# A down projection of mixture-of-experts blocks of at most 256 rows with its operands' roles exchanged

## Chip, cores and metric

The kernel runs on one core of a Trainium2 chip. The metric is the device time of one execution in microseconds (us); the profile is of one execution on that core.

## The reference

A block of a language model on 2048 tokens of width 1024. Three mixing branches (windowed attention, retention, attention to a memory) are computed, gated, merged and projected, and added to the input. What the change is about comes last:

```
logits = ht @ w_router + b_router                # 2048 tokens, 32 experts
top_vals, top_idx = lax.top_k(logits, 4)
gate = softmax(top_vals)
hid = ragged_dot(xs, w_up, group_sizes) + b_up   # 1024 -> 2048 per expert, rows sorted by expert
x_glu = minimum(hid[:, 0::2], 7.0)
x_lin = clip(hid[:, 1::2], -7.0, 7.0)
act = x_glu * sigmoid(1.702 * x_glu) * (x_lin + 1.0)
out = ragged_dot(act, w_down, group_sizes) + b_down      # 1024 -> 1024 per expert
y = zeros.at[tok].add(out * gate)
```

All of it is float32. Each product is formed from two parts of each operand, a high part rounded to the matmul's type (`_hi`) and the rest (`_lo`), in three passes: hi x hi, lo x hi and hi x lo.

## The kernel before

The kernel is a row of stages with a barrier between them. `project_mixers` projects the branches, `finish_mixing` finishes the mixing, routes the tokens and plans the blocks, and `run_experts` computes the experts from about 2356 us to the end.

**Blocks.** `finish_mixing` sorts the (token, expert) rows by expert, cuts each expert's rows into blocks of at most 384 (three tiles of 128) and sorts the blocks by size into seven width classes, `WIDTHS` (224, 240, 256, 272, 288, 304, 384). For each block a row of the table `blocks` holds the expert, the number of live tiles (`LIVE`), the first row, the number of tiles in the blocks before (`PRIOR`); the ends of the classes are in it too. `each_block` makes one loop for each class, so that the code of a block knows its width.

**One block on TensorE** (`pe`, from line 2650). A unit is a weight tile of 256 rows (`KU` = 2 chunks of 128) by 256 columns, 256 KB. A pair n is a group of 256 weight columns and has 4 units, m = 0 to 3. Pairs 0 to 7 (`UP` = 8) are the up projection, pairs 8 to 11 the down projection, 48 units in all. `unit` (lines 2630 to 2632) holds a 128 x 128 piece of the weights stationary and moves the block's rows, `width` columns at a time: 12 matmuls in a unit, results in two of the four banks `acc`, with output channels on the partitions. After the down projection, ScalarE adds the bias while it evicts a bank to `yT` (`take_down`, line 2427), TensorE turns `yT` back into rows (`turn_y`, line 2607, 4 transposes for a tile and half), and ScalarE multiplies them by the gate into `ys` (`gate`, line 2435). Half 0 (512 output channels) of a block is turned in pairs 10 and 11 of the same block, half 1 in pairs 0 and 1 of the next. POOL adds `ys` to the output by indirect DMAs (`scatter`).

**The next block's rows.** POOL gathers them into `xg`. TensorE turns them tile by tile into the one PSUM buffer `xT` (`turn_x`, line 2598, 8 transposes), ScalarE makes `x_hi` from it (line 2409), VectorE `x_lo` (line 2509). `turn_x` of tile i waits for `x_lo` of tile i - 1. The calls stand behind pair n = 7 (tile 0), n = 8 (tile 1) and n = 9 (tile 2):

```
if UP - 1 <= n < UP + 2:
    turn_x(following, n - UP + 1)
```

**The weights.** SyncE loads units in order into 8 raw buffers (`load`, line 2305), each as soon as the split eight units before it is done. ScalarE makes the high part `w_hi` (`split`, line 2403), VectorE `w_lo` (line 2503). 16 units are held (`HELD`); unit u goes where unit u - 16 was, and ScalarE waits for it by the semaphore `used`, which TensorE raises after each unit. In program order both engines split four pairs ahead: beside pair n they handle the units of pair n + 4, or those of the next block. When the up projection ends, all 16 units of the down projection fill the 16 places.

**The order on the engines** is written out by hand. VectorE for an up pair (from line 2561): read the first bank (`open_glu`, line 2514), split, read the second (`open_lin`, 2519), multiply by the sigmoid, split, multiply, split, the low part of the activations (`split_a`, 2536), split. ScalarE: split, sigmoid, two splits, `a_hi`, split. Both do `x` of tile 0 behind all eight pairs, and tiles 1 and 2 behind the third unit of pairs 8 and 9. TensorE's first matmul into a bank waits until the bank has been read (`free_bank`).

**Other places touched.** At the start of the stage POOL clears `yT` (line 2378) and ScalarE waits for it. In `project_mixers` ScalarE casts four weight chunks and then the first input tile (line 1578). In `finish_mixing` VectorE makes the columns of the table and TensorE sorts them.

## Time and profile before

| what | us |
|---|---|
| median of 3 runs (lowest to highest) | 4849.71 (4848.52 to 4853.77) |
| the profiled execution | 4852.9 |
| its span, first to last instruction | 4851.2 |

The profile gives for each engine its busy time: PE is TensorE's matmuls, PEld its weight loads, which overlap them, DVE VectorE, ACT ScalarE, POOL GpSimd; SPq is SyncE's queue of DMA issues. The timeline gives start, duration, engine, line, operation, output<-inputs, count, and in brackets the idle time of the engine before the instruction and what ended it. Matmuls overlap, so the distance between their starts is their price, and not their duration. PEclk is TensorE's granted clock as a share of 2.4 GHz.

### The profile page before, as it was taken

The page shows a single profiled execution, that of the slowest core. Times are in us where ns is not written, and L with a number is a line of the kernel's source. Part 1 is how long each engine was busy: PE and PEld are TensorE (multiplying, and loading weights), DVE is VectorE, ACT ScalarE, POOL GpSimd, SP SyncE. Part 2 cuts the span into 40 slices and gives each one's busy share as a digit, 9 for nine tenths or more (in the row PEclk, how much of TensorE's full clock was granted, in tenths as well). Part 3 has the DMA queues.
Part 4 walks back from the last instruction along what each step waited for, and adds up shares of the span by engine and source line. Part 5 has one row for each costly group of instructions (what it writes and reads, how often), then busy time and mean ns, then how long its engine had stood idle before and what let it go on. Part 6 is the DMA issues. An engine that isn't in the chain of part 4 may idle for free.

```text
span 4851.2 us, 98702 instructions
## 1 busy us (share of the span) xinstructions
PE 4650.1 (96%) x31230; PEld 4328.0 (89%) x31231; DVE 2937.2 (61%) x5403; ACT 2108.5 (43%) x3853; POOL 472.6 (10%) x455
## 2 busy tenths in 40 slices
PE   7999999999699899989699999999999999999997
PEld 6888888888477778878699999999999999999997
DVE  6555565555388644355566766666666666565654
ACT  4222221221377631222355555555555555555553
POOL 3000000000133100012200010001010110101000
PEclk9999999999799999999799999999999999999999
DMA  5333343232344443444476777676675767665654
GB/s 190 106 118 102 128 148 112 100 106 86 144 160 159 160 152 137 157 158 138 149 212 202 223 220 214 190 216 210 187 216 175 226 182 215 182 208 176 203 165 113
DMA packets 573959, 806.10 MB, mean 166 GB/s; under 512 B 51216, under 2 KB 516624, under 8 KB 566800
## 3 DMA queue, kind: packets, MB, share of 16 engines
q1 hardware_dynamic: 548032, 718.01, 45.1%
q0 software_dynamic: 25808, 86.59, 7.4%
q8 instruction: 65, 1.06, 0.1%
q14 instruction: 54, 0.44, 0.0%
HBM read 650.25 MB, written 154.21 MB: 166 GB/s over the span
## 4 chain that ended last, share of the span: by engine, by line
PE 50%; DMA 1%; DVE 0%; issue 0%; SPq 0%; ACT 0%; DVEq 0%; POOLq 0%; ACTq 0%
PE e_acc L2632 16%; PE e_acc L2630 16%; PE e_acc L2631 16%; PE e_xT L2598 2%; PE e_yp L2607 1%; DMA e_raw<-in_w_up 1%; DMA out<-e_ys,e_rec_out 0%; DVE e_wlo L2503 0%; DVEq L2254 0%; DVE e_xlo L2509 0%; ACT e_whi L2403 0%; SPq L2305 0%; POOLq L2198 0%; DVE e_lin L2519 0%; ACT e_ys L2435 0%
## 5 line engine op out<-in xcount | busy, mean ns | idle before, releaser
L2503 DVE TENSOR_TENSOR e_wlo<-e_raw,e_whi 128x512 fp32r<-128x512 f32 x1552 | 1055.7, 688 | 545.8 <-ACT e_whi L2403 529.2
L2630 PE MATMUL e_acc<-e_xhi,e_whi 128*128 128x272 f32 (+6 forms) x4096 | 1182.3, 289 | 3.6 <-DVEq L2558 2.6
L2632 PE MATMUL e_acc<-e_xlo,e_whi 128*128 128x272 f32 (+6 forms) x4096 | 1178.3, 288 | 0.0
L2631 PE MATMUL e_acc<-e_xhi,e_wlo 128*128 128x272 f32 (+6 forms) x4096 | 1176.6, 287 | 0.0
L2403 ACT CAST e_whi<-e_raw 128x512 fp32r<-128x512 f32 x1552 | 951.5, 647 | 196.8 <-DMA e_raw<-in_w_up 160.0
L2630 PEld LDWEIGHTS e_acc<-e_xhi,e_whi 128*128 128x128 f32 x4096 | 774.0, 189 | 4.6 <-issue 3.0
L2631 PEld LDWEIGHTS e_acc<-e_xhi,e_wlo 128*128 128x128 f32 x4096 | 775.6, 189 | 0.0
L2632 PEld LDWEIGHTS e_acc<-e_xlo,e_whi 128*128 128x128 f32 x4096 | 773.4, 189 | 0.0
L606 PE MATMUL p_acc<-p_hi,a_hi 128*128 128x464 f32 x1792 | 670.0, 374 | 6.9 <-DVE p_lo L508 6.9
L608 PE MATMUL p_acc<-p_hi,a_lo 128*128 128x464 f32 x1792 | 669.0, 373 | 0.0
L607 PE MATMUL p_acc<-p_lo,a_hi 128*128 128x464 f32 x1792 | 666.6, 372 | 0.0
L2630 PE MATMUL e_acc<-e_ahi,e_whi 128*128 128x272 f32 (+6 forms) x2048 | 598.9, 292 | 0.0
L2632 PE MATMUL e_acc<-e_alo,e_whi 128*128 128x272 f32 (+6 forms) x2048 | 588.6, 287 | 0.0
L2631 PE MATMUL e_acc<-e_ahi,e_wlo 128*128 128x272 f32 (+6 forms) x2048 | 587.5, 287 | 0.0
L475 ACT CAST p_hi<-p_raw 128x928 fp32r<-128x928 f32 x192 | 176.7, 969 | 638.7 <-PE p_acc L608 635.7
L2631 PEld LDWEIGHTS e_acc<-e_ahi,e_wlo 128*128 128x128 f32 x2048 | 387.5, 189 | 0.0
L2630 PEld LDWEIGHTS e_acc<-e_ahi,e_whi 128*128 128x128 f32 x2048 | 386.6, 189 | 0.0
L2632 PEld LDWEIGHTS e_acc<-e_alo,e_whi 128*128 128x128 f32 x2048 | 386.1, 189 | 0.0
L606 PEld LDWEIGHTS p_acc<-p_hi,a_hi 128*128 128x128 f32 x1792 | 336.9, 188 | 46.9 <-issue 7.1
L608 PEld LDWEIGHTS p_acc<-p_hi,a_lo 128*128 128x128 f32 x1792 | 336.6, 188 | 42.7
L607 PEld LDWEIGHTS p_acc<-p_lo,a_hi 128*128 128x128 f32 x1792 | 336.8, 188 | 40.8
L533 DVE TENSOR_TENSOR p_u<-p_acc,p_u 128x464 f32<-128x464 f32 x320 | 197.0, 638 | 262.5 <-PE p_acc L608 262.5
(331 smaller groups left out, 6247.0 us busy)
## 6 DMA issues: line engine op xcount, KB each, us to landing
e_raw<-in_w_up SPq DMA_DIRECT2D x1040, 256.0 KB, 3.2
e_raw<-in_w_down SPq DMA_DIRECT2D x512, 256.0 KB, 4.6
p_raw<-in_w_in SPq DMA_DIRECT2D x64, 928.0 KB, 4.9
z<-p_z SPq DMA_DIRECT2D x32, 928.0 KB, 4.0
z<-p_u SPq DMA_DIRECT2D x32, 928.0 KB, 3.9
b_gates<-z SPq DMA_DIRECT2D x16, 1536.0 KB, 7.0
oT<-x_oT SPq DMA_DIRECT2D x16, 1024.0 KB, 9.6
b_raw<-oT SPq DMA_DIRECT2D x16, 1024.0 KB, 9.6
```

The costliest lines, as they stand in the source:

```text
L475: act.copy(w_hi[slot(b, j)][:, ks, :], operand[j][:, ks, :]).then_inc(hi_made.sem, 1)
L533: dve.tensor_tensor(out[:, q, :], acc[slot(b, j)][q][:, 0:G], other[:, q, :], ALU.add).then_inc(added.sem, 1)
L606: pe.matmul(out, a_hi[:, j, at], hi[:, k, :], start=k == 0, stop=False)
L607: pe.matmul(out, a_hi[:, j, at], lo[:, k, :], start=False, stop=False)
L608: mm = pe.matmul(out, a_lo[:, j, at], hi[:, k, :], start=False, stop=k == HALF_K - 1)
L2403: act.copy(held(w_hi, u), loaded(u)).then_inc(hi_made.sem, 1)
L2503: dve.tensor_tensor(held(w_lo, u), loaded(u), held(w_hi, u).bitcast(F32), ALU.subtract).then_inc(lo_made.sem, 1)
L2598: mm = pe.transpose(xT[:, k * P:(k + 1) * P], xg[i][:, k * P:(k + 1) * P], ident[:])
L2607: mm = pe.transpose(yp[i % 2][:, j * P:(j + 1) * P], yT[half][:, j, i * P:(i + 1) * P], ident[:])
L2630: pe.matmul(out, whi, hi[:, k, 0:width], start=k == 0, stop=False)
L2631: pe.matmul(out, wlo, hi[:, k, 0:width], start=False, stop=False)
L2632: mm = pe.matmul(out, whi, lo[:, k, 0:width], start=False, stop=k == KD - 1)
```

## The change

For classes of at most 256 rows (`narrow`) the down projection holds the activations stationary (128 x 128 pieces of `a_hi` and `a_lo`, the last piece as wide as the rows left) and moves 512 weight columns, taken from two units at once (`rows_part`). One part is 12 matmuls and uses units m of two pairs. Its results have rows on the partitions: four banks, one for each half and tile. VectorE adds the bias row, which SyncE broadcasts by DMA to all partitions once a block (`add_row`, into `ya`), and ScalarE multiplies by the gate into `ys` (`gate_rows`). No `take_down` and no `turn_y` is done for these blocks; TensorE raises `y_turned` at the block's end instead. `used` rises by one behind each of the first three parts of a half and by five behind the fourth. `turn_x` of tiles 1 and 2 stands behind the first and second part. The table has a new column `LATE`, the live tiles of a block of the wider classes and 0 for a narrow one, which tells the next block whether transposes of half 1 are owed. POOL clears `ys`, and ScalarE waits for that. In `project_mixers` ScalarE waits, before it casts the first input tile, until the last outputs of the stage before are written. The diff, cut to its core:

```diff
@@ -1579,6 +1579,9 @@
 
             for n in range(KO):
                 if n == PARTS[0][1]:
+
+                    for written in weights.outputs_written:
+                        act.wait_ge(written.sem, written.after(TILES // 2 - 1))
                     split(0, 0, 0)
...
@@ -1685,10 +1688,12 @@
-EXPERT, LIVE, FIRST, COUNT, PRIOR, CUTS = range(6)
+EXPERT, LIVE, FIRST, COUNT, PRIOR, LATE, CUTS = range(7)
 WIDTHS = (224, 240, 256, 272, 288, 304, BLOCK_TILES * P)
 CLASSES = len(WIDTHS)
+NARROW = 3
+assert WIDTHS[NARROW - 1] <= 2 * P
...
+            link(dve.tensor_scalar(val[:, LATE:LATE + 1], over[:, NARROW:NARROW + 1], live, None, ALU.mult), False)
...
+        ya = sb("ya", [P, 2, 2, HALF])
+        down_row = sb("down_row", [P, D])
...
+        row_in, ys_cleared = sig("row_in", 16), sig("ys_cleared")
+        NARROW_TAKEN = ((3, 6), (7, 8))
...
-                if column == LIVE:
-                    self.live = self.get(LIVE, BLOCK_TILES)
+                if column == LIVE or column == LATE:
+                    self.live = self.get(column, BLOCK_TILES)
...
+                        sp.wait_ge(y_taken.sem, y_taken.after(b, 0))
+                        stand(sp, idle)
+                        sp.dma_start(down_row[:], io["b_down"][ds(e, 1), :].to_broadcast([P, D])).then_inc(row_in.sem, 16)
...
+            for t in ys:
+                pool.memset(t[:], 0.0).then_inc(ys_cleared.sem, 1)
...
+            def gate_rows(b, block, half, i, width):
+
+                rows = min(width - i * P, P)
+                act.wait_ge(y_taken.sem, y_taken.after(b, NARROW_TAKEN[half][i]))
+                act.wait_ge(rec_kept.sem, block.row)
+
+                act.wait_ge(y_sent.sem, block.prior * 16)
+                act.activation(ys[i][0:rows, half * HALF:(half + 1) * HALF], ya[0:rows, half, i, :], ACT.Copy,
+                               scale=rec_now[0:rows, i, 1:2].bitcast(F32)).then_inc(y_gated.sem, 1)
...
+            act.wait_ge(ys_cleared.sem, BLOCK_TILES)
...
+                narrow = width <= 2 * P
+                now = Block(act, b + 1)
+                if not narrow:
+                    before = Block(act, b, LATE, PRIOR)
                 for n in range(UP):
-                    if n == 0:
+                    if n == 0 and not narrow:
                         with before.tile(0):
                             gate(before, 1, 0)
                         with before.tile(1):
                             gate(before, 1, 1)
-                    if n == 1:
+                    if n == 1 and not narrow:
...
+                if narrow:
+                    stand(act, down_kept)
+                    for half in range(2):
+                        for m in range(PARTS - 1):
+                            split(*ahead(b, UP + 2 * half, m))
+                            if half == 0 and m < BLOCK_TILES - 1:
+                                with following.tile(m + 1):
+                                    split_x(following, m + 1, used.after(b, UP * PARTS))
+                        if half == 1:
+                            for i in range(2):
+                                with now.tile(i):
+                                    gate_rows(b, now, 0, i, width)
+                        split(*ahead(b, UP + 2 * half, PARTS - 1))
+                        if half == 1:
+                            for i in range(2):
+                                with now.tile(i):
+                                    gate_rows(b, now, 1, i, width)
+                        for m in range(PARTS):
+                            split(*ahead(b, UP + 2 * half + 1, m))
+                    continue
...
+            def add_row(b, half, i, width):
+                rows = min(width - i * P, P)
+                if i == 0:
+                    dve.wait_ge(summed.sem, summed.after(b, UP + 2 * half + 2))
+                else:
+                    dve.wait_ge(used.sem, used.after(b, (UP + 2 * half + 2) * PARTS))
+                dve.tensor_tensor(ya[0:rows, half, i, :], acc[2 * half + i][0:rows, :],
+                                  down_row[0:rows, half * HALF:(half + 1) * HALF], ALU.add).then_inc(
+                                      y_taken.sem, NARROW_TAKEN[half][i] - (NARROW_TAKEN[half][i - 1] if i else 6 * half))
...
+                if width <= 2 * P:
+                    dve.wait_ge(row_in.sem, row_in.after(b))
+
+                    dve.wait_ge(y_gated.sem, now.prior * 2 + 1)
+                    stand(dve, idle)
+                    for half in range(2):
+                        for m in range(PARTS - 1):
+                            split(*ahead(b, UP + 2 * half, m))
+                            if half == 0 and m < BLOCK_TILES - 1:
+                                with following.tile(m + 1):
+                                    split_x(following, m + 1)
+                        if half == 0:
+                            dve.wait_ge(x_lo_made.sem, following.prior + following.live + 1)
+                            dve.sem_inc(x_ready.sem, 1)
+                        for i in range(2):
+                            add_row(b, half, i, width)
+                        split(*ahead(b, UP + 2 * half, PARTS - 1))
+                        for m in range(PARTS):
+                            split(*ahead(b, UP + 2 * half + 1, m))
+                    continue
...
+            def rows_part(b, half, m, width):
+
+                for u in (UP + 2 * half, UP + 2 * half + 1):
+                    pe.wait_ge(lo_made.sem, lo_made.after(b, u * PARTS + m + 1))
+                first = 2 * half * PARTS + m
+                for kk in range(KU):
+                    k = m * KU + kk
+                    whi, wlo = (w[:, first:first + PARTS + 1:PARTS, kk, :] for w in (w_hi, w_lo))
+                    for i in range(2):
+                        if k == 0:
+                            free_bank(b, UP + half, i)
+                        cols = slice(i * P, min(width, (i + 1) * P))
+                        out = acc[2 * half + i][0:cols.stop - cols.start, :]
+                        hi, lo = a_hi[:, k, cols], a_lo[:, k, cols]
+                        pe.matmul(out, hi, whi, start=k == 0, stop=False)
+                        pe.matmul(out, hi, wlo, start=False, stop=False)
+                        mm = pe.matmul(out, lo, whi, start=False, stop=k == KD - 1)
+                        if k == KD - 1 and i == 0:
+                            mm.then_inc(summed.sem, 2)
+                mm.then_inc(used.sem, 1 if m < PARTS - 1 else PARTS + 1)
...
+                narrow = width <= 2 * P
                 pe.wait_ge(x_ready.sem, b + 1)
-                for n in range(PAIRS):
-                        if n == 0 and m == 1:
+                        if n == 0 and m == 1 and not narrow:
                             before = Block(pe, b, PRIOR)
-                        if n == 0 and m == 2:
-                            before.load(LIVE)
+                        if n == 0 and m == 2 and not narrow:
+                            before.load(LATE)
...
-                        if n == 0 and m == 3:
+                        if n == 0 and m == 3 and not narrow:
                             turn_y(before, 1, 0, y_taken.after(b, 0))
                             turn_y(before, 1, 1, y_taken.after(b, 0))
-                        if n == 1 and m == 2:
+                        if n == 1 and m == 2 and not narrow:
                             turn_y(before, 1, 2, y_taken.after(b, 0))
...
+                if narrow:
+                    for half in range(2):
+                        for m in range(PARTS):
+                            if half == 0:
+                                pe.wait_ge(a_lo_made.sem, a_lo_made.after(b, (m + 1) * KU))
+                            rows_part(b, half, m, width)
+                            if half == 0 and m < BLOCK_TILES - 1:
+                                turn_x(following, m + 1)
+                    for i in range(2):
+                        with now.tile(i):
+                            pe.sem_inc(y_turned.sem, 2)
```

## Rows read from the trace of the kernel before

**Rows 1.** The page, busy time and share of the span of each engine

```profile
PE 4650.1 (96%) x31230; PEld 4328.0 (89%) x31231; DVE 2937.2 (61%) x5403; ACT 2108.5 (43%) x3853; POOL 472.6 (10%) x455
```

**Rows 2.** Windows of the experts' stage: busy time, count, PEclk, DMA share

```profile
core 0: us, PE busy (x) PEld busy (x) DVE busy (x) ACT busy (x) POOL busy (x), PEclk, DMA share, GB/s
2380.00:4785.00 2405.00, 2404.03 (x19474) 2401.33 (x19474) 1564.02 (x2912) 1342.30 (x2549) 228.50 (x220) 1.00 0.67 201
```

**Rows 3.** Groups by form, up projection: count, busy us, mean ns

```profile
L2630 PE MATMUL e_acc<-e_xhi,e_whi 128*128 128x240 f32 x896 | 247.4, 276 | 0.0
...
L2630 PE MATMUL e_acc<-e_xhi,e_whi 128*128 128x256 f32 x640 | 181.2, 283 | 0.0
...
L2630 PE MATMUL e_acc<-e_xhi,e_whi 128*128 128x224 f32 x384 | 107.1, 279 | 3.3 <-DVEq L2558 2.6 <-DVE e_lin L2519 0.4 <-DVE e_glu L2514 0.3
```

**Rows 4.** Windows with matmuls alone, of 224, 240, 256 and 512 columns

```profile
2467.00:2492.00 25.00, 25.00 (x226) 25.00 (x226) 20.30 (x44) 14.54 (x30) 1.84 (x2) 1.00 0.90 280
2740.00:2765.00 25.00, 25.00 (x223) 25.00 (x223) 20.07 (x43) 13.84 (x28) 1.79 (x2) 1.00 0.90 284
3158.00:3183.00 25.00, 25.00 (x211) 25.00 (x210) 19.06 (x40) 13.44 (x27) 1.91 (x2) 1.00 0.90 277
1820.00:1920.00 100.00, 100.00 (x432) 80.58 (x431) 39.48 (x51) 18.71 (x8) 0.00 (x0) 1.00 0.40 140
```

**Rows 5.** Timeline of PE around the transposes of the outputs: start, us, line

```profile
3004.30 0.27 PE L2632 MATMUL e_acc<-e_xlo,e_whi 128*128 128x240 f32 x1
3004.41 1.04 PE L2607 MATMUL e_yp<-ident,e_yT 128*128 128x128 f32 x8
3005.20 0.36 PE L2630 MATMUL e_acc<-e_xhi,e_whi 128*128 128x240 f32 x1
3005.40 0.28 PE L2631 MATMUL e_acc<-e_xhi,e_wlo 128*128 128x240 f32 x1
```

**Rows 6.** Timeline of PE where a down projection of 240 columns begins

```profile
2974.40 1.04 PE L2598 MATMUL e_xT<-ident,e_xg 128*128 128x128 f32 x8
2975.19 0.36 PE L2630 MATMUL e_acc<-e_ahi,e_whi 128*128 128x240 f32 x1
...
2980.60 0.27 PE L2632 MATMUL e_acc<-e_alo,e_whi 128*128 128x240 f32 x1
2980.85 1.09 PE L2598 MATMUL e_xT<-ident,e_xg 128*128 128x128 f32 x8
```

**Rows 7.** Timelines of ACT and DVE in the same stretch

```profile
2978.52 1.02 ACT L2409 CAST e_xhi<-e_xT 128x1024 fp32r<-128x1024 f32 x1 [0.63 <-PE e_acc L2632]
...
2979.57 1.23 DVE L2509 TENSOR_TENSOR e_xlo<-e_xT,e_xhi 128x1024 fp32r<-128x1024 f32 x1 [0.95 <-ACT e_xhi L2409]
```

**Rows 8.** Timeline of PE in the last mixing stage, around an idle time

```profile
2092.45 1.03 PE L2131 MATMUL f_mT<-ident,f_mg 128*128 128x128 f32 x8
2096.05 0.47 PE L334 MATMUL f_acc<-f_whi,f_mhi 128*128 128x512 f32 x1 [2.56 <-DVE f_mlo L1969]
```

**Rows 9.** Window behind that idle time, columns as in rows 2

```profile
2096.80:2100.20 3.40, 3.40 (x9) 2.63 (x8) 2.22 (x12) 0.77 (x2) 0.00 (x0) 0.50 0.39 154
```

**Rows 10.** Timeline of DVE at the start of a block

```profile
3005.57 0.17 DVE L2565 COPY e_up_bias<-e_bias 128x16 f32 x1 [3.48 <-issue]
3005.88 0.47 DVE L2514 TENSOR_SCALAR e_glu<-e_acc,e_up_bias 128x240 f32<-128x240 f32 x1
```

**Rows 11.** Timeline at the start of the experts' stage

```profile
2362.41 2.71 POOL L2378 MEMSET e_yT<- 128x1536 f32 x2
...
2366.62 0.65 ACT L2403 CAST e_whi<-e_raw 128x512 fp32r<-128x512 f32 x1 [8.88 <-issue]
...
2371.08 1.01 ACT L2409 CAST e_xhi<-e_xT 128x1024 fp32r<-128x1024 f32 x1
```

**Rows 12.** DMA issues between 1689 and 1691 us, last number us to landing

```profile
oT<-x_oT SPq DMA_DIRECT2D x1, 1024.0 KB, 4.2
```

**Rows 13.** Timeline of ACT at the opening of the projection of the mixers

```profile
1697.92 1.90 ACT L1578 CAST b_ohi<-b_raw 128x2048 fp32r<-128x2048 f32 x1 [2.51 <-DMA b_raw<-oT]
```

More of the change, by code:

```diff
@@ L2451, in _ @@
             for b, width in each_block(act):
-                before, now = Block(act, b), Block(act, b + 1)
+                narrow = width <= 2 * P
+                now = Block(act, b + 1)
+                if not narrow:
+                    before = Block(act, b, LATE, PRIOR)
                 for n in range(UP):
-                    if n == 0:
+                    if n == 0 and not narrow:
                         with before.tile(0):
@@ L2475, in _ @@
                     down_kept.sem, 1)
-                act.wait_ge(down_kept.sem, b + 1)
+                act.wait_ge(down_kept.sem, down_kept.after(b))
                 for n in range(UP, PAIRS):
@@ L2650, in _ @@
             for b, width in each_block(pe):
+                narrow = width <= 2 * P
                 pe.wait_ge(x_ready.sem, b + 1)
-                for n in range(PAIRS):
+                for n in range(UP if narrow else PAIRS):
                     for m in range(PARTS):
-                        if n == 0 and m == 1:
+                        if n == 0 and m == 1 and not narrow:
                             before = Block(pe, b, PRIOR)
-                        if n == 0 and m == 2:
-                            before.load(LIVE)
+                        if n == 0 and m == 2 and not narrow:
+                            before.load(LATE)
                         if n == 2 and m == 0:
```

## The prediction

> **What bounds the kernel now.** I read the page's busy line first, then the windows, then the groups by form, then the timeline around one block. The page has TensorE busy 96% of the span [rows 1]. The windows sharpen this: from 2380 to 4785 us the experts' stage runs, and TensorE is busy 2404.0 of 2405 us at the full clock (2.4 GHz), VectorE 65% and ScalarE 56%, DMA at 0.67 [rows 2]. So every microsecond taken from or added to TensorE's own sequence there moves the end, and work of the other engines counts only where TensorE comes to wait for it.
>
> How many blocks does the change touch? An up projection issues 128 matmuls of each of its three lines per block, and the groups of line 2630 have 384, 896 and 640 of them at 224, 240 and 256 columns [rows 3]: 3, 7 and 5 blocks, 15 of the 32. The wider 17 keep their path.
>
> **Part A, the matmuls.** A narrow block's down projection is now 8 column groups x 8 chunks x 3 passes = 192 matmuls of `width` moving columns; it becomes 2 halves x 8 chunks x 2 row tiles x 3 = 96 of 512. The price is the distance from start to start. Four windows in which nothing but matmuls runs give it [rows 4]; each count holds about two that straddle the edges. 25 us / 224 = 111.6 ns at 224 columns, 25 / 221 = 113.1 at 240, 25 / 209 = 119.6 at 256, and 100 us / 430.5 = 232 ns at 512 columns (stage before, same three passes, stationary 128 x 128, full clock). New: 96 x 232 = 22.27 us. Old: 21.43, 21.72, 22.96. The differences are +0.84 x 3, +0.55 x 7, -0.69 x 5 = +2.9 us. Halving the number of matmuls buys nothing, because the columns streamed are 49,152 against 43,008 to 49,152.
>
> A rule of the Trainium skill speaks for much more: TensorE: Matmul & The Clock Gate, section "Back-to-back issue gap", puts a sustained stream of weight load and matmul at about 131 ns for 512 columns, and by it the 96 would take 12.6 us and the kernel would gain over 100 us. The row at 512 columns says 232, so the sum stands as above.
>
> **Part B, the transposes of the outputs.** They go for narrow blocks: one pair of tiles (8 transposes) for half 0 and one for half 1, the latter in the next block. One pair: last matmul at 3004.30, transposes at 3004.41, the next matmuls at 3005.20 and 3005.40, where two steps of 0.113 would have done [rows 5]: 1.10 - 0.23 = 0.87 us. 30 x 0.87 = -26.1 us, all of it on the bounding engine. ScalarE's gates had waited for these; they are replaced by as many gates from SBUF.
>
> **Part C, a transpose of the next block's rows that comes too early.** Transposing input tile i needs the one xT buffer, so it waits for `x_lo` of tile i-1. Tile 0 is turned at the end of the up projection (2974.40), the down projection starts at 2975.19, and tile 1 is turned behind pair n = 8, at 2980.85 [rows 6]. In the new order tile 1 is turned behind `rows_part(0, 0)`, that is behind 12 matmuls: 2975.19 + 0.09 + 12 x 0.232 = 2978.06. What must be there is `x_lo` of tile 0: ScalarE makes x_hi at 2978.52 to 2979.54, VectorE x_lo at 2979.57 to 2980.80 [rows 7]. Both stand behind the last gate chain and the last weight splits of the up projection, in the order that the change leaves as it is. So TensorE waits from 2978.06 to 2980.85, 2.79 us. Today's order just fits: its last matmul started 2980.60, a wait of 0.14. Net +2.65. The other blocks repeat this: the turn of tile 1 stands 5.58 to 5.67 us behind the first down matmul in all ten blocks of 224 and 240, and in the five of 256 x_lo is ready 5.65 to 5.67 behind it. That gives +2.58 (224), +2.65 (240), +2.84 (256); 3, 7 and 5 times: +40.5 us. Nothing hides it, since TensorE has no other work in its queue behind the waiting transpose. This is the largest term.
>
> **Part D, the clock.** Before each turn TensorE would stand 2.5 us without work, and with the transposes there are 3.5 us between matmuls. The nearest row is in the stage before: transposes from 2092.45, then idle 2.56 us, matmuls from 2096.05 [rows 8]; then 3.4 us in which the granted clock is 0.50 (1.2 GHz, the lower level) and only 8 whole matmuls fit, 0.42 each instead of 0.232 [rows 9]. Lost: 3.4 - 8 x 0.232 = 1.54 us. That gap and mine are alike (3.6 us between matmuls there). Ends: never 0, every time 15 x 1.54 = 23 us. One row can't say how often; I take every second time, +11.5. The same page of the Trainium skill, in its table "Why this matters for your kernels", warns only of idle gaps longer than these; by that the term would be 0, but the row shows a fall behind one of 2.56 us.
>
> **Small parts.** Bias row: SyncE issues one more DMA per block (512 KB beside 12 MB of weights) behind unit 23 of the up projection, waiting for the previous block's last bank to be read, long done by then; VectorE needs the row some 25 us later, so 0. Behind it on SyncE's queue stand the loads of units 24 and on, eight units ahead of their split. VectorE gains four adds of 512 columns per block (each about as long as one of the 48 weight splits, also 512 columns) and ScalarE loses eight evictions; VectorE is 65% busy. The last two adds fall at the block's end, together with five splits that the new credits of `used` release at once. VectorE then reaches the next block's first bank late: today 3005.88, 6.9 us into the block (whose 48th matmul is the one at 3004.30), after 3.48 us in which it only loads registers [rows 10]; with two adds more and the splits bunched there I estimate two us more, some 9.1. TensorE needs that bank at pair 2, 10.8 us in, and its second at 11.2, which VectorE frees at about 10.6. The cover is about half a microsecond; 0 taken, up to +0.5 per block kept. TensorE's two `sem_inc` per block have no row; between 0 (the sequencer runs ahead) and one transition like the 0.09 above each, +2.7 in all; 0 taken. Start of the stage: POOL clears ys too, three tiles of 1024 columns, as many as the two of 1536 that took 2.71 us, and ScalarE waits for it; its first cast goes from 2366.62 to about 2369.3, but the three casts behind it waited for weights anyway, so x_hi at 2371.08 slips by only about 0.6 [rows 11]. With the planner's extra operation and column, +1.0. The new wait at the opening of the projection of the mixers: the last 1 MB of outputs is issued between 1689 and 1691 and lands 4.2 us later, by 1695.2 [rows 12], and ScalarE stands idle at this place for 2.51 us, until 1697.92, for another DMA [rows 13]: 0, at most +1 if the two waits should add.
>
> **Sum.** +2.9 - 26.1 + 40.5 + 11.5 + 1.0 = +29.8 us. The profiled execution is 4852.9 (span 4851.2), 3.2 above the median of the three runs (4849.7); against the median that gives 4879.5.
>
> **Rivals.**
> - *The clock holds.* Same stalls, term D at 0: +18.3, 4868. For it: a turn of 8 transposes ends each gap, and one row is thin. Against: that same row. Chance 0.22.
> - *The next block's first banks come late too*, or the clock falls every time. VectorE's backlog at the block's end outgrows its half microsecond, or 15 falls: +36 to +50, 4886 to 4900. Chance 0.15.
> - *Faster: the stall isn't there.* If x_lo of tile 0 were ready before 2978.06, or the turn cost TensorE nothing, A, B and the start alone would remain: 2.9 - 26.1 + 1.0 = -22.2, 4827.5. It decides by the wait: with no clock loss, the break-even is a net wait of 22.2 / 15 = 1.5 us per block instead of 2.65. For it: VectorE idles 0.95 us ahead of x_lo. Against: that idling is for ScalarE's x_hi, and ScalarE's sequence ahead of x_hi is untouched and starts when the up projection ends. A second way to this side is the 512 columns streaming faster from the two-part weight tile: at 213 ns, 96 x 19 ns x 15 = -27 us. Chance together 0.09.
> - *No change*, a wait half as long or the faster stream against the stalls: within 9.7 us. Chance 0.06.
> - That the new path isn't taken can be left out: the counts at three widths say it is, in 15 blocks.
>
> **How the numbers follow.** The forecast (stalls with the clock falling at part of them) has 0.48. This kernel's measurement can tell 0.2% (9.7 us) from no change. Slower by more: 0.48 + 0.22 + 0.15 = 0.85; within: 0.06; faster: 0.09. The range must hold 8 in 10: from the clock holding, less a few us for the rate of 512 columns (232 might be 229 in this stage, -4), to falls every time with some of the small terms: 4863 to 4896. It leaves out the faster side, the no-change cases and the far end of the late banks.
>
> **What would show it.** Right: TensorE in the experts' stage no longer at 100%; a wait of the transposes on `x_lo` of some 2.8 us, 15 times, about 42 us in the list of waits; matmuls of 512 columns 0.232 us apart; TensorE at half clock for a few us behind some of the waits; a narrow block's down phase near 26 us against 23.7 for 240 columns, its up phase 0.87 shorter. Wrong: no such wait (then A and B stand alone and the kernel is faster), 512 columns off 232 ns, or waits on VectorE's reads of the first banks of a block.

## The result, and the profile after

The changed kernel takes 4927.6 us (median of 5 runs, 4925.1 to 4935.4) against 4852.4 for the kernel before, run beside it: a ratio of 1.0158, with a 95% interval of 1.0147 to 1.0169, or 75 us more. The forecast was slower by 29.8 us, 4879.5, with a range of 4863 to 4896. The direction was right, the size was not, and the result lies outside the range. The profiled execution has a span of 4924.6 us, 73.4 more than the one before.

The page first, its busy line:

```profile
PE 4653.9 (95%) x29552; PEld 4243.8 (86%) x29553; DVE 2968.5 (60%) x5464; ACT 2062.1 (42%) x3718; POOL 483.6 (10%) x458
```

TensorE's busy time hardly changed against [rows 1] (4650.1), so the time went into idle time. Windows of the experts' stage say where, the 15 narrow blocks first and the 17 wide ones behind them. The columns are those of [rows 2].

```profile
core 0: us, PE busy (x) PEld busy (x) DVE busy (x) ACT busy (x) POOL busy (x), PEclk, DMA share, GB/s
2380.00:3472.00 1092.00, 1048.53 (x7443) 965.76 (x7443) 747.62 (x1430) 571.14 (x1051) 95.13 (x88) 0.98 0.70 210
3472.00:4860.00 1388.00, 1361.01 (x10363) 1354.22 (x10362) 847.92 (x1543) 724.71 (x1362) 140.34 (x132) 1.00 0.65 195
```

Before, TensorE was busy 2404.0 of 2405 us. Now it stands 43 us in the narrow blocks, and 27 in the wide ones, whose code on TensorE the change left alone. From the first matmul of the first narrow block to that of the first wide one it takes 3472.38 - 2378.66 = 1093.7 us against 1052.8, +40.9; from there to the end of the span it is 1452.2 against 1419.6, +32.6. The two make up the 73.4. TensorE's own list of waits, from 2390 to 4800 us, names two causes (us in total, times, longest):

```profile
PE e_xT L2678 <- DVE e_xlo L2559: 39.6, 15, 2.9
PE e_acc L2731 <- DVE e_lin L2569: 30.0, 34, 1.7
```

**The wait on x_lo** is part C. The timeline of TensorE in a block of 240 columns, where [rows 6] shows the kernel before:

```profile
2998.53 0.48 PE L2713 MATMUL e_acc<-e_whi,e_ahi 128*128 128x512 f32 x1
...
3001.17 0.40 PE L2715 MATMUL e_acc<-e_whi,e_alo 128*112 128x512 f32 x1
3004.16 1.09 PE L2678 MATMUL e_xT<-ident,e_xg 128*128 128x128 f32 x8 [2.60 <-DVE e_xlo L2559]
3005.01 0.48 PE L2713 MATMUL e_acc<-e_whi,e_ahi 128*128 128x512 f32 x1
```

The twelfth matmul of the first part starts at 3001.17, 2.64 us behind the first, and the transposes of tile 1 start at 3004.16: 5.63 us behind the first matmul, as in every block before (5.58 to 5.67 at these widths). The wait is 2.60 us by the profile, 15 such waits add up to 39.6 us.

**The clock.** This is another block of 240 columns, and then a window in it:

```profile
2928.76 0.40 PE L2715 MATMUL e_acc<-e_whi,e_alo 128*112 128x512 f32 x1
2931.77 1.97 PE L2678 MATMUL e_xT<-ident,e_xg 128*128 128x128 f32 x8 [2.61 <-DVE e_xlo L2559]
2933.39 0.78 PE L2713 MATMUL e_acc<-e_whi,e_ahi 128*128 128x512 f32 x1
2933.97 0.63 PE L2714 MATMUL e_acc<-e_wlo,e_ahi 128*128 128x512 f32 x1
...
2935.07 0.40 PE L2714 MATMUL e_acc<-e_wlo,e_ahi 128*112 128x512 f32 x1
```

```profile
2932.00:2935.00 3.00, 3.00 (x12) 2.69 (x12) 0.49 (x2) 1.01 (x1) 0.00 (x0) 0.53 0.30 94
```

The same wait, but then eight transposes take 1.62 us until the next matmul instead of 0.85, and matmuls stand 0.42 to 0.58 apart instead of 0.232, until about 2934.8; the granted clock of the window is 0.53, so most of it ran at the lower level, 1.2 GHz. Eleven of the fifteen narrow down phases show it, with a granted clock of 0.94 over the phase: two of 224 columns, four of 240 (27.5 to 27.6 us against 25.9 and 26.1 without) and all five of 256. Four do not (1.00). The expectation of `later` below says ten; the trace of the changed kernel has eleven.

**The wide blocks** were the surprise. Here is SyncE's queue in the up projection of a block of 272 columns, in the changed kernel and then at the same place in the kernel before:

```profile
3644.27 0.37 SPq L2320 DMA_DIRECT2D e_rec_in<-slots  x1
3645.00 0.34 SPq L2346 DMA_DIRECT2D e_down_row<-in_b_down  x1
3645.59 10.19 SPq L2315 DMA_DIRECT2D e_raw<-in_w_up  x8
```

```profile
3600.99 0.37 SPq L2310 DMA_DIRECT2D e_rec_in<-slots  x1
3601.62 5.35 SPq L2305 DMA_DIRECT2D e_raw<-in_w_up  x8
```

SyncE stands at this place until POOL has taken over the records, in both kernels. Its own list of waits in the wide blocks of the kernel before has:

```profile
SPq L2331 <- POOL e_rec_now L2387: 168.6, 17, 13.9
```

The loads behind it, held back, then go out at once. In the changed kernel the broadcast goes ahead of them: the first load is issued 1.32 us behind the records instead of 0.63, and the eight loads take 10.2 us to issue instead of 5.4. In the other blocks of 272 to 304 columns behind the first it is 7.6 to 10.7 against 5.1 to 8.5. ScalarE and TensorE, some 10 us later:

```profile
3646.41 0.67 ACT L2419 CAST e_whi<-e_raw 128x512 fp32r<-128x512 f32 x1
3655.43 0.64 ACT L2419 CAST e_whi<-e_raw 128x512 fp32r<-128x512 f32 x1 [8.35 <-DMA e_raw<-in_w_up]
```

```profile
3657.26 0.39 PE L2731 MATMUL e_acc<-e_xhi,e_whi 128*128 128x272 f32 x1 [1.14 <-DVE e_lin L2569]
```

ScalarE waits 8.35 us for the first of these weight tiles. In these fifteen blocks its longest wait for one is 7.5 to 8.4 us, before 2.0 to 3.8. Over all the wide blocks its list of waits has, before and after (us in total, times, longest):

```profile
ACT e_whi L2403 <- DMA e_raw<-in_w_up: 127.6, 82, 3.8
```

```profile
ACT e_whi L2419 <- DMA e_raw<-in_w_up: 183.6, 57, 8.4
```

So ScalarE stood for these loads before the change too, and TensorE didn't; now it stands 56 us longer, and some of it reaches TensorE. VectorE's split stands behind ScalarE's cast, and its reading of the second bank (`open_lin`) behind that split, so TensorE waits for the bank. An up projection of 272 columns takes 51.4 to 53.8 us instead of 50.3 to 51.0. In the first wide block (49.5 us against 49.8) and the last, of 384 columns (69.15 in both), no loss shows.

### The profile page after: what moved, and what is told of

It is laid out like the page before. It is cut to its first block, busy times and chain, and to the rows that moved or that the text cites. A ratio compares the mean times of both kernels' runs of the same rounds, so it can differ in the third digit from the quotient of the medians.

```text
span 4924.6 us, 94881 instructions
## 1 busy us (share of the span) xinstructions
PE 4653.9 (95%) x29552; PEld 4243.8 (86%) x29553; DVE 2968.5 (60%) x5464; ACT 2062.1 (42%) x3718; POOL 483.6 (10%) x458
## 4 chain that ended last, share of the span: by engine, by line
PE 41%; DMA 4%; DVE 2%; issue 2%; ACT 1%; DVEq 1%; SPq 1%; ACTq 0%; POOL 0%; POOLq 0%
PE e_acc L2731 11%; PE e_acc L2733 11%; PE e_acc L2732 11%; DMA e_raw<-in_w_up 4%; PE e_acc L2713 2%; PE e_acc L2714 2%; PE e_acc L2715 2%; PE e_xT L2678 1%; PE e_yp L2687 1%; DVEq L2264 1%; DVE e_wlo L2553 1%; SPq L2315 0%; ACT e_whi L2419 0%; DVE e_xlo L2559 0%; DVE e_lin L2569 0%
## 5 line engine op out<-in xcount | busy, mean ns | idle before, releaser
L2731 PE MATMUL e_acc<-e_ahi,e_whi 128*128 128x272 f32 (+3 forms) x1088 | 328.8, 302 | 0.0
L2733 PE MATMUL e_acc<-e_alo,e_whi 128*128 128x272 f32 (+3 forms) x1088 | 322.0, 296 | 0.0
L2732 PE MATMUL e_acc<-e_ahi,e_wlo 128*128 128x272 f32 (+3 forms) x1088 | 321.7, 296 | 0.0
L508 DVE TENSOR_TENSOR p_lo<-p_raw,p_hi 128x928 fp32r<-128x928 f32 x192 | 207.2, 1121 | 91.8 <-ACT p_hi L475 91.8
L2429 ACT ACTIVATE e_sg<-e_glu 128x272 f32<-128x272 f32 (+6 forms) x256 | 109.6, 428 | 289.6 <-DVE e_glu L2564 289.6
L334 PE MATMUL b_acc<-b_hi,b_ohi 128*128 128x512 f32 x512 | 203.1, 397 | 17.6 <-DVE b_olo L1609 16.0
```

The lines of the kernel that those rows point to most:

```text
L334: pe.matmul(out, x_hi(k), w_hi(k), start=first, stop=False)
L508: dve.tensor_tensor(w_lo[slot(b, j)][:, ks, :], operand[j][:, ks, :], w_hi[slot(b, j)][:, ks, :].bitcast(F32), ALU.subtract).then_inc(lo_m ...
L2731: pe.matmul(out, whi, hi[:, k, 0:width], start=k == 0, stop=False)
L2732: pe.matmul(out, wlo, hi[:, k, 0:width], start=False, stop=False)
L2733: mm = pe.matmul(out, whi, lo[:, k, 0:width], start=False, stop=k == KD - 1)
```

## Experiments

All times are medians; ratios are to the kernel before in the same job. Differences to the changed kernel are between medians of different jobs, in which the kernel before had 4851.1 to 4853.0 us, so they are good to a microsecond or two. The diffs are cut to their core: the runs that start from the kernel before also declare `down_row` and its semaphore, and before_tiny also waits for the last of these DMAs at the end of the program.

**before_row: the kernel before, plus the broadcast.**

```diff
                         load_records(b + 2)
+                        sp.wait_ge(y_taken.sem, y_taken.after(b, 0))
+                        stand(sp, idle)
+                        sp.dma_start(down_row[:], io["b_down"][ds(e, 1), :].to_broadcast([P, D])).then_inc(row_in.sem, 16)
```

> The kernel before, with one thing of the change added: SyncE's broadcast of the bias row (512 KB) behind unit 23 of every block; nobody reads it. In the changed kernel the 17 wide blocks, whose code on TensorE is the old one, take 32.6 us more from the first wide up projection to the end of the span (1419.6 to 1452.2 us), all of it in their up projections, where SyncE's eight held-back weight loads stand behind this DMA. Theory 'broadcast': this kernel loses the same, +30 to +38 us, in the wide blocks, and at most +5 in the 15 narrow ones. Rival 'something else of the change' (register loads, the LATE column, buffers at other addresses): within 5 us of before.

4885.5 against 4851.2, ratio 1.0067 (1.0050 to 1.0084): +34 us. The narrow blocks are as before to a tenth (45.2 us up, 23.7 to 23.8 down at 240 columns), and seven of the eight up projections at 272 columns take 52.0 to 53.6. From the first wide block to the end it is 1455.4 us, 35.9 more than before; some 3 of these belong to one block of 288 columns (57.6 us against 54.8 in the others), in which the clock also fell. TensorE's waits in the wide blocks:

```profile
PE e_acc L2636 <- DVE e_lin L2525: 19.8, 21, 1.7
PE e_acc L2636 <- issue: 5.1, 4, 1.5
```

The one DMA, read by nobody, reproduces the whole loss of the wide blocks. In the narrow blocks the same DMA costs nothing. Why was not tested by a run of its own, but the traces show a difference. By the code, SyncE is let go after two tiles of gathered rows there instead of three. In the kernel before it passes the place 8.7 to 9.1 us into a narrow block (11.5 in the first), and 14.2 to 15.5 us into a wide one of 272 to 304 columns. Two such blocks begin at 2930.01 and 3586.78:

```profile
2938.84 0.37 SPq L2310 DMA_DIRECT2D e_rec_in<-slots  x1
```

```profile
3600.99 0.37 SPq L2310 DMA_DIRECT2D e_rec_in<-slots  x1
```

One wide block is let go early too, the first one, at 9.4 us. It loses nothing by the broadcast (49.81 us up in both kernels). That speaks for the time at which SyncE gets there and against the width, but no run shows it. (The last block, of 384 columns, is let go at 18.5 us and loses nothing either; its up projection lasts 69 us.)

**narrow_row: the changed kernel, broadcast in narrow blocks only.**

```diff
-                        sp.wait_ge(y_taken.sem, y_taken.after(b, 0))
-                        stand(sp, idle)
-                        sp.dma_start(down_row[:], io["b_down"][ds(e, 1), :].to_broadcast([P, D])).then_inc(row_in.sem, 16)
+                        with sp.If(now.get(LATE, BLOCK_TILES) < 1):
+                            sp.wait_ge(y_taken.sem, y_taken.after(b, 0))
+                            stand(sp, idle)
+                            sp.dma_start(down_row[:], io["b_down"][ds(e, 1), :].to_broadcast([P, D])).then_inc(row_in.sem, 16)
```

> The changed kernel with the broadcast only in the blocks that read it (LATE is 0). Theory 'broadcast': the wide blocks' up projections return to 50.6 us at 272 columns (53.5 in the changed kernel), and the time falls by 30 to 36 us, to about 4894. Rival 'something else of the change': stays at about 4927.

4903.6, ratio 1.0104 (1.0088 to 1.0121): 24 us off the changed kernel, not 33. Behind the first wide block the up projections at 272 columns take 50.6 to 52.0. From the first wide block to the end it is 1430.8 us, still 11.3 more than before. Only the register load and the branch are left at this place, and they put the first held-back load off from 0.63 us behind the issue of the records to 1.48 or 1.49:

```profile
3562.49 0.37 SPq L2320 DMA_DIRECT2D e_rec_in<-slots  x1
3563.97 5.61 SPq L2315 DMA_DIRECT2D e_raw<-in_w_up  x8
```

The rest of the change is in the wide blocks of `moved` below as well, and those lose nothing. So the loads have no slack here, whatever it is that delays them.

**before_tiny: the kernel before, plus a DMA of 4 KB at that place.**

```diff
                         load_records(b + 2)
+                        sp.wait_ge(y_taken.sem, y_taken.after(b, 0))
+                        stand(sp, idle)
+                        sp.dma_start(down_row[0:1, :], io["b_down"][ds(e, 1), :]).then_inc(row_in.sem, 16)
```

> The kernel before with a DMA of the bias row to one partition (4 KB) at the place where the broadcast (512 KB) stood in before_row, and nothing else. If the broadcast costs by the data it moves ahead of the eight held-back weight loads, this is near 0 to +8 us (the issue alone: SyncE reaches the loads about 0.6 us later in each of 17 wide blocks). If it costs by anything that stands between SyncE's release and the loads, +30 us as in before_row. The run narrow_row, whose wide blocks had only a register load and a branch there, and no DMA, lost 11.2 us in them, so I expect between: +5 to +15.

4860.0 against 4851.1, ratio 1.0017 (1.0007 to 1.0027): +8.8 us, of which TensorE's list of waits in the wide blocks shows this:

```profile
PE e_acc L2637 <- DVE e_lin L2526: 4.9, 5, 1.3
```

Here the first held-back load is issued 1.26 us behind the records, 0.63 later than before, and from the first wide block to the end it is 7.0 us more. So a delay of the loads alone costs about a quarter of before_row's loss at 0.63 us and a third at the 0.86 of narrow_row. The rest comes with what the broadcast has more than the small DMA: 512 KB ahead of eight loads of 256 KB, in more packets.

**before_moved: the kernel before, plus the full broadcast behind unit 39.**

```diff
                         load_records(b + 2)
+                    if u == 10 * PARTS - 1:
+                        sp.wait_ge(y_taken.sem, y_taken.after(b, 0))
+                        stand(sp, idle)
+                        sp.dma_start(down_row[:], io["b_down"][ds(e, 1), :].to_broadcast([P, D])).then_inc(row_in.sem, 16)
```

> The kernel before with the full broadcast in every block, but behind unit 39 (the last of up pair 5's span of the queue), where the held-back loads have caught up. Theory 'it stands ahead of loads that have no slack': within 3 us of before, against +34 in before_row. Rival 'it costs DMA time wherever it stands': +15 to +34.

4851.7 against 4851.1, ratio 1.0002 (0.9993 to 1.0011). The same bytes in the same blocks, 16 units further on in the queue, cost nothing, and TensorE shows no wait in the wide blocks. The loss is one of place. The part of the expectation that named an up pair for the place was loose: unit 39 is a down unit in the queue, and its DMA is issued 28 to 41 us into a block, while TensorE is in the up projection.

**moved: the changed kernel, broadcast behind unit 39.** The edit is the one line `if u == 10 * PARTS - 1:` ahead of the three of the broadcast.

> The changed kernel with the broadcast behind unit 39 instead of unit 23, still in every block. The wide blocks return to their times of before (50.6 us for an up projection at 272 columns), the waits on x_lo and the falls of the clock stay: 32 to 36 us off, about 4893. If narrow blocks need the row sooner than that, VectorE waits on row_in and the narrow down phases grow.

4890.4, ratio 1.0085 (1.0069 to 1.0100): 37 us off the changed kernel. The up projections at 272 columns are back at 50.4 to 50.8, and the narrow down phases are unchanged (25.9 to 28.2 before the last), so the row arrives in time. Again eleven of them fall to the lower clock, but in part other blocks of 240 columns.

**later: the changed kernel, tiles 1 and 2 of the next block one part later.**

```diff
-                            if half == 0 and m < BLOCK_TILES - 1:
-                                with following.tile(m + 1):
-                                    split_x(following, m + 1, used.after(b, UP * PARTS))
+                            if half == 0 and m > 0:
+                                with following.tile(m):
+                                    split_x(following, m, used.after(b, UP * PARTS))
...
-                            if half == 0 and m < BLOCK_TILES - 1:
-                                with following.tile(m + 1):
-                                    split_x(following, m + 1)
+                            if half == 0 and m > 0:
+                                with following.tile(m):
+                                    split_x(following, m)
...
-                            if half == 0 and m < BLOCK_TILES - 1:
-                                turn_x(following, m + 1)
+                            if half == 0 and 0 < m < BLOCK_TILES:
+                                turn_x(following, m)
```

The three places are ScalarE's, VectorE's and TensorE's programs.

> The changed kernel with the transposes of the next block's tiles 1 and 2, and the two engines' splits of them, one part later (behind the second and third part of half 0). Theory 'too early': the wait on x_lo (43.8 us in 16 waits) goes, and with it the ten stretches at half clock in the narrow blocks; a 240-column block's down phase goes from 26.1 or 27.5 us to 23.4 to 23.6. -40 - 15 us: about 4872. Rival 'the wait only moves', to the third part or to the next block's start: 4900 to 4927.

4869.3, ratio 1.0037 (1.0022 to 1.0051): 58 us off the changed kernel, where 55 were expected. The transposes now follow the 24th matmul without a wait, and no narrow down phase runs at half clock:

```profile
2770.47 0.40 PE L2714 MATMUL e_acc<-e_wlo,e_ahi 128*128 128x512 f32 x1
2770.71 0.40 PE L2715 MATMUL e_acc<-e_whi,e_alo 128*128 128x512 f32 x1
2770.94 0.40 PE L2713 MATMUL e_acc<-e_whi,e_ahi 128*112 128x512 f32 x1
2771.18 0.39 PE L2714 MATMUL e_acc<-e_wlo,e_ahi 128*112 128x512 f32 x1
2771.41 0.40 PE L2715 MATMUL e_acc<-e_whi,e_alo 128*112 128x512 f32 x1
2771.64 1.07 PE L2678 MATMUL e_xT<-ident,e_xg 128*128 128x128 f32 x8
2772.47 0.48 PE L2713 MATMUL e_acc<-e_whi,e_ahi 128*128 128x512 f32 x1
```

A down phase of 240 columns takes 23.3 us, the up projections stay at 44.5 to 45.3.

**filler: the changed kernel with 11 matmuls inside the wait.**

```diff
                             rows_part(b, half, m, width)
+                            if half == 0 and m == 0:
+                                pe.wait_ge(lo_made.sem, lo_made.after(b, (UP + 1) * PARTS + 2))
+                                for _ in range(11):
+                                    pe.matmul(yp[0][:], a_hi[:, 0, 0:P], w_hi[:, 1:PARTS + 2:PARTS, 0, :], start=True, stop=True)
                             if half == 0 and m < BLOCK_TILES - 1:
                                 turn_x(following, m + 1)
```

> The changed kernel with 11 extra matmuls of 512 columns (results unused, 2.55 us) inside TensorE's wait of 2.79 us ahead of the transpose of tile 1. The end of the wait is set by x_lo and stays. Theory 'idle time drops the clock': no stretch at half clock in the narrow blocks' down phases, all of them 26.0 us instead of 26.1 or 27.5: -15 us, about 4912. Rival 'the clock falls for another reason, or its fall costs nothing on the path': 4925 to 4930.

4912.0, ratio 1.0122 (1.0105 to 1.0139): 15.5 us off the changed kernel, with more work in it. The wait on x_lo is filled, and what follows runs at full clock:

```profile
2926.66 0.39 PE L2715 MATMUL e_acc<-e_whi,e_alo 128*112 128x512 f32 x1
2926.89 2.74 PE L2795 MATMUL e_yp<-e_whi,e_ahi 128*128 128x512 f32 x11
2929.64 1.09 PE L2678 MATMUL e_xT<-ident,e_xg 128*128 128x128 f32 x8
2930.49 0.48 PE L2713 MATMUL e_acc<-e_whi,e_ahi 128*128 128x512 f32 x1
2930.80 0.39 PE L2714 MATMUL e_acc<-e_wlo,e_ahi 128*128 128x512 f32 x1
```

All narrow down phases of 224 and 240 columns are 25.9 to 26.1 us, those of 256 are 26.3 to 27.2 (27.9 to 28.8 in the changed kernel). In the traces the narrow blocks take 15.8 us less than in the changed kernel and their down phases 16.6 less, some 1.5 us for each of the eleven falls. That is the clock's share: a down phase without a fall is as long in both kernels (26.1 us at 240 columns).

**moved_later: both repairs.** The edits of moved and later together.

> Both repairs in the changed kernel: the broadcast behind unit 39, and the transposes of tiles 1 and 2 one part later. The two causes sit in different blocks (wide and narrow) and should add: 4869.3 (the run later) less 33 = 4836, that is 12 to 17 us faster than the kernel before. What is left against before should be parts A and B alone: +2.9 - 26.1 + 1, plus about 5 for VectorE's late first banks.

4835.3 against 4851.1, ratio 0.9968 (0.9957 to 0.9980): 16 us faster than the kernel before. The causes add: later (4869.3) and 37 us for the place of the broadcast would give 4832. What is left on TensorE is a short wait at the second bank of pair 2. Waits, then VectorE, then TensorE in a block of 240 columns that begins at 2855.1:

```profile
PE e_acc L2731 <- DVE e_lin L2569: 2.2, 7, 0.4
```

```profile
2865.00 0.17 DVE L2625 COPY e_up_bias<-e_bias 128x16 f32 x1 [4.70 <-issue]
2865.32 0.47 DVE L2564 TENSOR_SCALAR e_glu<-e_acc,e_up_bias 128x240 f32<-128x240 f32 x1
...
2866.31 0.46 DVE L2569 TENSOR_SCALAR e_lin<-e_acc,e_up_bias 128x240 f32<-128x240 f32 x1
```

```profile
2866.22 0.27 PE L2733 MATMUL e_acc<-e_xlo,e_whi 128*128 128x240 f32 x1
2866.82 0.38 PE L2731 MATMUL e_acc<-e_xhi,e_whi 128*128 128x240 f32 x1 [0.33 <-DVE e_lin L2569]
```

The list of waits counts little, 2.2 us in 7, because it takes a matmul as busy until its modelled end. The distance from start to start says more: 0.60 instead of 0.113, and then 0.22. VectorE reads the first bank 10.2 us into the block and the second at 11.2.

**gates_last: moved_later with ScalarE's last two gates behind its bunched splits.**

```diff
-                        if half == 1:
-                            for i in range(2):
-                                with now.tile(i):
-                                    gate_rows(b, now, 1, i, width)
                         for m in range(PARTS):
                             split(*ahead(b, UP + 2 * half + 1, m))
+                        if half == 1:
+                            for i in range(2):
+                                with now.tile(i):
+                                    gate_rows(b, now, 1, i, width)
```

> The run moved_later with ScalarE's two gates of half 1 behind its five bunched weight splits instead of between the first and the second. In moved_later TensorE stands about 0.5 us at the second bank of pair 2 of each narrow block of 224 and 240 columns, because VectorE reads that bank only 11.3 us into the block: its splits wait for ScalarE's casts, and those stand behind the gates. Theory 'VectorE's late first banks': VectorE starts about 1.3 us earlier, the up projections at 240 columns go from 44.9 to 44.3, and the time falls by 3 to 5 us, to about 4831. Rival: the 4.7 us in which VectorE loads registers set the time, and nothing changes (4835).

4828.8 against 4853.0, ratio 0.9950 (0.9937 to 0.9964): 24 us faster than the kernel before, 6.5 below moved_later (5.5 in the narrow blocks of the two traces, 8.3 if each is taken against the kernel before of its own job). VectorE in a block that begins at 2850.24:

```profile
2857.62 0.17 DVE L2625 COPY e_up_bias<-e_bias 128x16 f32 x1 [3.38 <-issue]
2857.95 0.47 DVE L2564 TENSOR_SCALAR e_glu<-e_acc,e_up_bias 128x240 f32<-128x240 f32 x1
```

It reads the first bank 7.7 us into the block instead of 10.2. All up projections of 240 columns take 44.31 us. VectorE's stretch of register loads shrank too, from 4.70 to 3.38 us, so the rival was wrong in taking it as fixed.

## Why the prediction was wrong, point by point

The traces give the narrow blocks as a chain of kernels, from the first matmul of the stage to the first one of the wide blocks: 1052.8 us before, 1029.5 in gates_last, and 1093.7 in the changed kernel. The last step, +64.3, is +5.8 in the up projections and +58.5 in the down phases; of these filler has 41.9, and 16.6 go with the clock.

- **What bounds the kernel** was read right: TensorE's own sequence. The mistake is in what was taken to have cover.
- **Part A**, +2.9 us, and **part B**, -26.1: right, -23.2 in all against -23.4 measured (gates_last, where TensorE waits for 0.4 us in the whole stage by its list). Behind the first block an up projection is 0.87 to 0.88 us shorter at each width, as forecast. The down phases agree less well one by one: from A and half of B, -0.03, -0.32 and -1.56 us at 224, 240 and 256 columns were to be expected, and -0.3, -0.4 to -0.5 and -1.3 were measured. In part the old waits of 0.1 to 0.2 us account for it, and in the sum the errors cancel, which is luck. The matmuls of 512 columns stand 0.232 apart, as forecast from the stage before [rows 4], and a down phase of 240 columns is 23.3 us. The 131 ns that the Trainium skill gives (TensorE: Matmul & The Clock Gate, section "Back-to-back issue gap") are shown by no run here.
- **Part C**, +40.5: right, 41.9 measured (the forecast is net of the short old waits at this place, which the -23.4 holds). Predicted 2.79 us from 2978.06 to 2980.85; the profile has 2.60, since it counts the last matmul as busy until its modelled end. Start to start, which the term was made of, the transposes stand 5.63 us behind the first matmul, as forecast. Without the wait, and with the full clock that comes with that, the kernel (later) is 58 us faster.
- **Part D**, +11.5 for half of the 15 waits: the mechanism right and the price of one fall too (1.5 us), the number of falls too low. Eleven fell, and that makes 15.5 (filler, by the medians) to 16.6 us. The Trainium skill (TensorE: Matmul & The Clock Gate, "Why this matters for your kernels") warns only of longer idle times than these; here the clock fell behind one of 2.6 us.
- **Small parts: the step that failed is the bias row.** "VectorE needs the row some 25 us later, so 0. Behind it on SyncE's queue stand the loads of units 24 and on, eight units ahead of their split." The first half held, the second did not. The cover named was eight units ahead of the split, but SyncE comes to this place only when POOL has taken over the records, in the wide blocks behind the first 14.2 us and more after their start. The raw buffers have run low by then: in the wide blocks of the kernel before ScalarE already waits 127.6 us for weights. TensorE was spared by a margin that no view prints, but that list of waits was there to be asked about. The broadcast took that margin: +34 us in before_row, +0.6 in before_moved. The text counted what waits behind the new DMA in units of the queue, and not in microseconds. It also gave the change's effect on the 17 wide blocks no term at all, since "the wider 17 keep their path"; it was 32.6 us.
- **VectorE's late first banks**: 0 taken, +0.5 per block as bound. The up projections of the narrow blocks are 5.8 us longer in all than in gates_last: 0.2 to 1.0 us in nine of the ten of 224 and 240 columns, 0.6 in the first of 256 and nothing in the others. The estimate of 9.1 us into the block was 9.8 to 10.8. Whether the start of the stage costs the 1.0 us of the sum can't be seen: the first matmul stands at 2378.66 against 2378.80, and between 2374.3 and 2381.1 in the eleven traces.
- **The sum with the sizes as measured** (against the kernel before, by the traces): A and B -23.4, C +41.9, D +16.6, late banks +5.8, together +40.9 in the narrow blocks; +32.6 from the wide ones. The spans differ by 73.4 and the medians by 75. With the broadcast where it is harmless the forecast of 29.8 stands against 39.2 (moved: 4890.4 against 4851.1), inside the range.
- **The rivals.** "The clock falls every time, or late banks" had the right extras, but none had the wide blocks, and so the range ended 32 us short. The faster side was real, but as a repair: 4828.8 was measured where the rival had 4827.5.

Open: why, of the ten waits of 2.6 us at 224 and 240 columns, six brought the clock down and four did not (the five at 256, of 2.7 to 2.9 us, all did). In `moved` it was eleven again, but not the same blocks, and the runs here tell only that it needs the idle time. And whether what before_row loses beyond the delay is the bytes on the DMA engines or the packets (144 for a broadcast by the totals of the two pages, 2 for the small DMA); before_tiny changes both.

## What to carry to other kernels

An instruction added to a queue is priced by what stands behind it at the moment the queue gets there, not by how late its own consumer comes. Put it where the queue has caught up (here 16 loads later it was free), and look at every class of blocks that runs through that queue. When a loop body gets coarser steps (12 matmuls for two units instead of one), count again, in microseconds, every hand-placed wait in it: the transposes kept their step number and lost half their distance. And filling a wait with useless matmuls is a cheap way to tell what the wait costs from what the clock costs behind it.

## What was not expected of the hardware

A register load and a branch on SyncE, without any DMA, cost 11 us over the 17 wide blocks, where they put the loads off by 0.86 us each time (narrow_row). Transposes behind an idle time of 2.6 us ran at the lower clock too: 1.62 us for eight instead of 0.85. The width of the stationary operand did not matter: in the fence of `later`, pieces of 112 columns (2770.94 to 2771.64) stand 0.23 apart like those of 128.
